# Two-layer encoder trunk: the order of work around projected query chunks in layer 1, and of one weight chunk in layer 0

## What is computed

```python
def encoder_trunk(x, rel_bias, norm_mix, norm_ffn, a_w_in, ..., moe_w_down):
    for i in range(DEPTH):
        h = rms_norm(x, norm_mix[i])
        j = i // N_MIXERS
        if i % N_MIXERS == 0:
            x = x + dilated_attention(h, a_w_in[j], a_q_gain[j], a_k_gain[j], a_w_out[j], rel_bias)
        else:
            x = x + local_gqa_attention(h, b_w_in[j], b_q_gain[j], b_k_gain[j], b_sink[j], b_w_out[j], rel_bias)
        h = rms_norm(x, norm_ffn[i])
        x = x + expert_choice_ffn(h, moe_router[i], moe_w_gate[i], moe_w_up[i], moe_w_down[i])
    return x
```

## Time and profile before

| | |
|---|---|
| median of three runs | 1865.71 us |
| the profiled execution | 1863.89 us |
| its span, from the first instruction to the last | 1862.1 us |
| PE busy | 1768.5 us (95%) |
| DVE, ACT, POOL busy | 1330.7, 1132.3, 236.5 us |
| mean granted PE clock | 0.981 of full speed |
| attention units of layer 1 | about 1028 to 1190 us |
| attention units of layer 0 | begin at about 80 us |

### The profile page before, as it was taken

The page is one execution under the profiler, slowest core; times in us unless marked ns, Lnnn a source line. Parts: engine busy times, 40 slices in busy tenths (PEclk is TensorE's granted clock), DMA queues, the critical chain, the costliest instruction groups (busy, mean ns, idle before and its releaser), DMA issues.

```text
span 1862.1 us, 24459 instructions
## 1 busy us (share of the span) xinstructions
PE 1768.5 (95%) x10260; PEld 1394.6 (75%) x10260; DVE 1330.7 (71%) x1008; ACT 1132.3 (61%) x1185; POOL 236.5 (13%) x118
## 2 busy tenths in 40 slices
PE   6989989999999999999989888998999999999997
PEld 5888889977767767767679776897767767767765
DVE  4624455678888888888845445548888888888885
ACT  4443452457777777777744445433777777777774
POOL 0100000000110100100011000001121211211311
PEclk9989999999999999999999899899999999999999
DMA  4311123499999999999962111228999999999994
GB/s 157 89 55 55 41 69 105 162 351 368 387 374 395 387 375 395 386 377 390 344 166 80 38 35 32 79 100 293 366 377 387 383 380 390 387 380 392 380 391 144
DMA packets 155841, 486.00 MB, mean 261 GB/s; under 512 B 12199, under 2 KB 46119, under 8 KB 155687
## 3 DMA queue, kind: packets, MB, share of 16 engines
q1 hardware_dynamic: 148308, 459.26, 66.1%
q0 software_dynamic: 7424, 25.17, 5.8%
HBM read 454.26 MB, written 30.13 MB: 260 GB/s over the span
## 4 chain that ended last, share of the span: by engine, by line
PE 87%; DVE 5%; ACT 3%; DMA 2%; issue 1%; POOL 0%; SPq 0%; POOLq 0%; DVEq 0%; ACTq 0%
PE ps L1760 19%; PE ps L1762 19%; PE ps L1761 19%; PE ps L1463 5%; PE ps L1465 4%; PE ps L1464 4%; PE ps L1543 3%; PE ps L1650 2%; PE ps L1652 2%; PE ps L1651 2%; PE ps L1419 2%; PE ps L1731 1%; PE ps L1515 1%; PE ps L1724 1%; PE ps L1532 1%
## 5 line engine op out<-in xcount | busy, mean ns | idle before, releaser
L1274 DVE TENSOR_TENSOR w_lo<-ring,w_hi 128x2048 fp32r<-128x2048 f32 x384 | 876.5, 2290 | 153.2 <-ACT w_hi L989 153.0
L989 ACT ACTIVATE w_hi<-ring 128x2048 fp32r<-128x2048 f32 x384 | 736.3, 1918 | 276.2 <-PE ps L1762 268.1
L1760 PE MATMUL ps<-w_hi,xe_hi 128*96 128x512 f32 x1016 | 403.5, 397 | 0.0
L1762 PE MATMUL ps<-w_hi,xe_lo 128*96 128x512 f32 x1016 | 399.4, 393 | 0.0
L1761 PE MATMUL ps<-w_lo,xe_hi 128*96 128x512 f32 x1016 | 398.0, 392 | 0.0
L1762 PEld LDWEIGHTS ps<-w_hi,xe_lo 128*96 128x96 f32 x1016 | 163.8, 161 | 71.5
L1760 PEld LDWEIGHTS ps<-w_hi,xe_hi 128*96 128x96 f32 x1016 | 163.8, 161 | 69.5 <-DVE xe_lo L1373 5.6
L1761 PEld LDWEIGHTS ps<-w_lo,xe_hi 128*96 128x96 f32 x1016 | 164.3, 162 | 64.6
L1760 PE MATMUL ps<-w_hi,hid_hi 128*96 128x512 f32 x512 | 201.6, 394 | 0.0
L1463 PE MATMUL ps<-c_hi,hT_hi 128*128 128x256 f32 x648 | 189.4, 292 | 12.5 <-ACT qraw L791 6.5
L1762 PE MATMUL ps<-w_hi,hid_lo 128*96 128x512 f32 x512 | 201.1, 393 | 0.0
(11 more groups left out here) (190 smaller groups left out, 2171.8 us busy)
## 6 DMA issues: line engine op xcount, KB each, us to landing
ring<-in_moe_w_gate SPq DMA_DIRECT2D x128, 1024.0 KB, 7.5
ring<-in_moe_w_up SPq DMA_DIRECT2D x128, 1024.0 KB, 8.9
ring<-in_moe_w_down SPq DMA_DIRECT2D x128, 1024.0 KB, 9.0
wbuf<-in_a_w_in SPq DMA_DIRECT2D x9, 1024.0 KB, 8.7
ffn_rows<-hrow SPq DMA_DIRECT2D x12, 512.0 KB, 2.7
wbuf<-in_b_w_in SPq DMA_DIRECT2D x5, 1024.0 KB, 7.9
unit_rows<-row SPq DMA_DIRECT2D x36, 132.0 KB, 1.8
bias<-bias_rows SPq DMA_DIRECT2D x4, 768.0 KB, 10.1
```

The lines of the kernel that those rows point to most:

```text
L989: nc.scalar.activation(w_hi[:, n % SPLIT], ring[:, n % RAW], ACT.Copy).then_inc(hi_split, 1)
L1274: nc.vector.tensor_tensor(w_lo[:, n % SPLIT], ring[:, n % RAW], w_hi[:, n % SPLIT].bitcast(F32), ALU.subtract).then_inc(lo_split, 1)
L1760: nc.tensor.matmul(out, hi[:, k, :], w_hi[:, n % SPLIT, i, cols], start=(k == 0), stop=False)
L1762: ins = nc.tensor.matmul(out, lo[:, k, :], w_hi[:, n % SPLIT, i, cols], start=False, stop=(k == KM - 1))
```

## The change

**Layer 1, PE.** The projected q tiles alternate between banks 7 and 6, and wait for the copy of the tile two before (the first one for all before it). A wait for the rows of the group before is added ahead of them. In unit 6 all six tiles stand in the middle of the unit, ahead of `times_v`. Behind the tiles, PE waits until five of the six have been copied out. In units 10 to 16 three idle products stand between the next scores and `times_v`, and ten in unit 17.

**Layer 1, ACT.** In unit 0, `exps(1)` comes ahead of the four tiles in the middle, the high half of group 2's q behind the first of them, and `exps(2)` behind the second. In unit 6, `exps(8)` comes behind the second of the six.

**Layer 1, DVE.** `head_squares` comes in units 0 and 6 themselves, right behind the logits, each half as soon as its three tiles are there. `scale_heads` stays in units 2 and 8, with the row copy of the same unit between its two multiplications. The low half of the next output chunk moves one unit later.

**Layer 0.** Chunk 3 is loaded ahead of the wait for the bias table. ACT writes its high half behind the first three copies of transposed q, DVE its low half between the squares and the scaling of k. ACT writes the high half of chunk 4 one unit later, behind `fold_high` and `exps(2)`.

```diff
 def proj_bank(n):
+    if CHUNKS[n // NT][0] and beside(n // NT):
+        return 7 - n % 2
     return 6 if beside(n // NT) else 6 + n % 2
...
 def tiles_placed(layer, n):
     if layer and n == 0:
         return tiles[:2], tiles[2:], []
+    if layer:
+        return [], tiles, []
     return [], tiles[:1], tiles[1:]
...
 # SP
     sp.dma_start(tab_ap, tab).then_inc(tab_out, 16)
+    load_chunk(3)
     sp.wait_ge(tab_out, 16)
...
-            chunk = 3
+            chunk = 4
...
 # ACT
         take_pair("q", b)
+    high_chunk(first + 3)
     for t in range(4):
         take_tile(first + 2, t)
...
+    early = layer == 1 and len(tiles_between) > 1
+    if early and n == 0:
+        exps(1)
-    for c, t in tiles_between:
+    for j, (c, t) in enumerate(tiles_between):
         take_tile(c, t)
+        if early and n == 0 and j == 0:
+            high_chunk(first + 4)
+        for m in between if early and j == 1 else []:
+            exps(m)
     for lot in batches[2:]:
         take_lot(lot)
-    if layer == 0 and n == 0:
-        high_chunk(first + 3)
     if layer == 0 and n == 1:
         fold_high((3, 2, 1, 0))
-    if layer and n == 0:
-        exps(1)
     for m in ahead + between:
-        exps(m)
-    for c in ended_before(layer, n):
-        high_chunk(c + 2)
+        if not early:
+            exps(m)
+    for c in ended_before(layer, n) if layer or n > 1 else ended_before(layer, 0) * n:
+        if layer == 0 or n:
+            high_chunk(c + 2)
...
 # DVE
-def head_squares(kind):
+def head_squares(kind, chunk=None):
     for i in range(2):
+        if chunk is not None:
+            dve.wait_ge(qkv_taken, NT * qkv_before(chunk) + (i + 1) * NT // 2)
...
-def scale_heads(kind):
+def scale_heads(kind, between=None):
     step(nc.vector.tensor_tensor(heads, heads, hrstd..., ALU.mult), head_sums)
+    if between is not None:
+        between()
     nc.vector.tensor_tensor(heads, heads, head_gain..., ALU.mult).then_inc(head_normed, 1)
...
         head_squares(kind)
+        if layer == 0 and kind == "k":
+            low_chunk(first + 3)
         scale_heads(kind)
...
+    seam = layer == 1 and n < 2 * NT and n % NT in (2, 3)
-    if n:
+    if n and not (seam and n % NT == 3):
         take_unit(n - 1)
     for m in ahead + between:
         logits(m)
-    if layer == 0 and n == 0:
-        low_chunk(first + 3)
-    for c in ended_before(layer, n - 1) if n else []:
-        if n > 1 and n % NT and CHUNKS[c][1] in "qk":
+    if layer and n < 2 * NT and n % NT == 0:
+        head_squares("q", chunk_at(layer, "q", n // NT + 1))
+    if seam and n % NT == 2:
+        scale_heads("q", lambda: take_unit(n))
+    for c in ended_before(layer, n - 1 - (layer and n % NT == 3)) if n else []:
+        if layer and n % NT == 2:
+            continue
+        if layer == 0 and n > 1 and n % NT and CHUNKS[c][1] in "qk":
             scale_heads(CHUNKS[c][1])
         low_chunk(c + 2)
     for c in ended_before(layer, n):
-        if n and CHUNKS[c][1] in "qk":
+        if layer == 0 and n and CHUNKS[c][1] in "qk":
...
 # PE, project
-    m = r - 1 if beside(chunk) or t == 0 and beside(chunk - 1) else r - 2
+    m = r - 1 if (beside(chunk) and layer == 0) or t == 0 and beside(chunk - 1 + layer) else r - 2
+    if layer and beside(chunk):
+        pe.wait_ge(row_ready, layer * NU + (CHUNKS[chunk][2] - 1) * NT)
...
 # PE, middle of a unit, behind scores(n+2)
     for c, t in tiles_between:
         project(c, [t])
+    if layer and tiles_between:
+        pe.wait_ge(qkv_taken, NT * qkv_before(tiles_between[-1][0]) + NT - 1)
     if dense:
         idle_products(1)
+    if layer and n > 2 * NT - 3:
+        pe.wait_ge(qkv_taken, NT * qkv_before(FIRST_OUT[layer]))
+        idle_products(10 if n == NU - 1 else 3)
```

## The result

The changed kernel takes 1845.44 us (median of 4 runs, 1842.61 to 1849.5); the kernel before takes 1865.81 beside it. The ratio is 0.9897, with a 95% interval of 0.9885 to 0.9908: about 19 us faster, against a forecast of 1842 and a range of 1834 to 1855. The profiled execution took 1845.36 us with a span of 1843.5, so 18.6 us of span went.

What follows compares the result with a forecast made beforehand. PE, holding 87% of the chain, was taken as the bound, so its waits in attention blocks are paid in full. Terms 11.0 + 8.6 + 0.9 + 1.6 = 22.1 us off 1863.89 gave 1841.8, forecast 1842, range 1834 to 1855.

Steps and rivals of the forecast that it cites:

- Two banks: Layer 1, units 0 and 6: each tile that need not wait for the copy saves 0.77 us, 3.0 + 3.1 in all.
- Units 0 to 4: Layer 1 up to `scores(6)`: 11.0 us gained, counted as 3.0 + 7.5 + 0.5, the 3.0 being the banks'.
- The two waits: Layer 1, units 1 and 2: PE's waits of 1.73 and 1.52 us for exponentials and the copy behind them go.
- the store's wait: Layer 1, unit 4: DVE's maximum waits 3.2 us for the store of row 0, issued behind a chunk's load.
- the third wait: Layer 1, unit 3: PE's 3.13 us for row copy and scaling, said to be traded almost whole for DVE's store wait.
- Units 6 to 10: Layer 1 on to `scores(12)`: banks 3.1, row-copy waits 6.2, half clock 2.9, less 3.6 of new waits: 8.6 us gained.
- both new waits: Layer 1: PE waits about 1.3 us at unit 8 behind a high half, about 2.3 ahead of `scores(12)` for the heads.
- Units 10 to 17: Layer 1's end: half clock goes (2.0 + 1.6 + 0.5 us), idle products cost 0.75 and 2.5: +0.9 us gained.
- The slower rival: Layer 1, units 10 to 17: idle products, with PE at half clock throughout, make it 17 us slower, 1881; chance 0.05.
- Layer 0: Up to its second projected tile 4.3 us gained; half clock behind a new 3.5 us wait costs 2.7; net +1.6.
- DVE 4.28 before the scaling of k: Layer 0: DVE's 4.28 us of idle time there was to cover chunk 3's low half (2.3 us).
- The low bound: Layer 0's worst case: net -2.4 us, with 13 us of half clock, as at 1058.

## Why the prediction was right, step by step

The measured 1845.4 us lies in the range, 3.4 above the forecast. In the profile 18.6 us of span went instead of 22.1: layer 1 gave 20.4 of 20.5, layer 0 gave 0.2 of 1.6, and the start came 2.5 us late. That layer 1 comes so close is luck in part, since its last term changes from one execution to the next.

*Two banks*: right, 2.88 us a tile and 3.0 in the first group measured alone. In the second group 7.6 us hung on the bank instead of 3.1; the half clock there is the likely cause.

*Units 0 to 4*: 10.2 of 11.0. The two waits went, 1.2 (forecast 1.4) came, and the store's wait was found where and about as long as forecast: 3.59 for 3.2, and the profile shows 3.1 us to be had by moving it. The chain on DVE behind it is right, too: `logits(5)` ends at 1073.98, and the forecast's 1072.3 with the 1.9 us of later start is 1074.2. One remark failed: the third wait was not "traded almost whole", the order on DVE gave 3.7 there. And one of the forecast's own signs of being wrong came: half clock in units 3 and 4, from 1070 to 1081. It cost little, as the forecast had argued for that case, since most of it hides behind the store: the stretch is 0.8 longer than forecast.

*Units 6 to 10*: 8.3 of 8.6, with both new waits as forecast (1.22 for 1.3, 2.35 for 2.3). That the clock stays up behind them held in this execution and not in the next one of the same kernel; most of what it cost there falls into the stretch behind (50.3 us for 47.7).

*Units 10 to 17*: the term +0.9 was 1.9 in this profile, and this is the execution's luck. In the eleven profiles with the products the stretch took 47.7 to 50.6 us, against 49.6 before, so against before the stage gives between +1.9 and about -1. The term was sized by the wrong comparison. It took the stage without products to be that of before, at half clock for 9 us; ahead of it layer 1 had changed, and without products the clock is at half three times. Against the changed kernel without them the products are worth 5.0 to 7.6. The slower rival named the opposite of what the products do here.

*Layer 0*: the step that failed, hidden by the total. The wait of 3.42 ahead of the second tile (3.5 forecast) came as argued, and with it, in six of seven profiles, the half clock behind it. But up to that tile 2.5 us were gained, not 4.3. What did not hold is "DVE 4.28 before the scaling of k" as cover for the low half: that idle time was POOL at work, and work put beside it made POOL 1.97 longer. The half clock then takes 2.3 (2.7 forecast), and 0.2 are left; where the clock stayed up, 2.5. So +1.6 lies between two outcomes and is neither. The low bound has a slip besides: 4.3 less half of 13 is -2.2, not -2.4. With the cover mended, and the ACT order behind it, layer 0 gives 7.3 us against before.

Ahead of all edits the changed profile is 2.5 us late (44.56 against 42.08). The clock is at half for a part of 33 to 37 us there (0.57, against 1.00 before), and single matmuls of the first projected tile take 0.41 us until 21.8 us, where before they fall to 0.28 at 20.5. The forecast, made on one profile, could not see that.

## What to carry to other kernels

Idle time of an engine is cover only if what it waits for does not slow when the engine works: look at the releaser of that wait, and price the new work beside it. When a stage's clock is argued from the profile of before, ask what the stage will look like after all other edits, for a repair that looks nearly worthless may hold the clock up. Landmarks inside one execution settle terms of 2 us that medians, here spread over 7 us, cannot, as long as the clock was the same in both: up to layer 0's second tile seven executions agree within 0.1 us, and the next tile alone differs by 2.3.

## What the runs showed that was not expected

hrstd is held off by one DVE instruction of two operands, or a copy, that is under way when it begins, to within 0.15 us of its end; one that begins 0.8 us later does it no harm.

The same wait of PE has either sequel. In layer 0's first tiles PE waits 2.06 us for DVE in both kernels. Before:

```profile
31.03 1.09 PE L1431 MATMUL ps<-ident,v 128*128 128x128 f32 x8 [2.06 <-DVE v L1089]
```
```profile
33.00:37.00 4.00, 4.00 (x37) 4.00 (x36) 1.49 (x2) 1.24 (x3) 0.00 (x0) 1.00 0.00 0
```

After:

```profile
32.14 1.09 PE L1453 MATMUL ps<-ident,v 128*128 128x128 f32 x8 [2.06 <-DVE v L1101]
```
```profile
33.00:37.00 4.00, 3.81 (x21) 3.61 (x19) 2.60 (x3) 1.02 (x1) 0.00 (x0) 0.57 0.00 0
```

No edit lies ahead of this place on PE. With layer 0's edits undone the window shows 0.70, in the second execution of the changed kernel 0.79. What decides between 2.4 and 1.2 GHz behind such a wait stays open.
